# GpSimd starts the second chunk's weight low part only behind VectorE's eight low parts of the norm, in both transitions of a one-core decoder kernel

## What is computed

```python
x = x + rmsnorm(mix, prm['g_post_mix'][layer])
h = rmsnorm(x, prm['g_pre_ffn'][layer])
f = swiglu(h, prm['w_gate_d'][i], prm['w_up_d'][i], prm['w_down_d'][i])
x = x + rmsnorm(f, prm['g_post_ffn'][layer])
if layer == N_A_LAYERS - 1:
    kv = rmsnorm(x, prm['g_kv']) @ prm['w_kv']
```

## Time and profile before

| | |
|---|---|
| time, median of 3 runs | 1826.3 us (1825.19 to 1826.43) |
| profiled execution: own time, span | 1821.79 us, 1820.0 us |
| granted TensorE clock, mean | 0.957 of full speed |
| TensorE busy (matmuls) | 1693.2 us, 93% |
| VectorE, ScalarE, GpSimd busy | 943.6, 745.8, 539.9 us (52%, 41%, 30%) |
| mean DMA rate | 155 GB/s |

### The profile page before, as it was taken

How to read it: one execution, slowest core, us unless ns; L and a number is a source line. 1 busy time by engine, 2 the same in 40 slices (tenths; PEclk the granted TensorE clock), 3 DMA queues, 4 the chain that set the end, 5 groups by cost and what they waited for, 6 DMA issues and landing times.

```text
span 1820.0 us, 29086 instructions
## 1 busy us (share of the span) xinstructions
PE 1693.2 (93%) x11312; PEld 1537.1 (84%) x11312; DVE 943.6 (52%) x1161; ACT 745.8 (41%) x977; POOL 539.9 (30%) x326
## 2 busy tenths in 40 slices
PE   6898797999999998989898998899999999999988
PEld 5898687999999997889666486899898988989886
DVE  6796534211111001322486423877686776868686
ACT  6354453322222122321355222554454554545454
POOL 1001223355554444242000021352331524324161
PEclk8899888999999999999898999899999999999989
DMA  6623202144445342121532415579799796977961
GB/s 206 123 85 131 70 24 70 47 144 144 144 144 181 103 144 86 47 93 60 193 129 84 151 59 130 175 249 297 205 268 232 227 273 208 290 207 237 252 238 49
DMA packets 346267, 281.96 MB, mean 155 GB/s; under 512 B 9505, under 2 KB 311117, under 8 KB 346055
## 3 DMA queue, kind: packets, MB, share of 16 engines
q1 hardware_dynamic: 324947, 251.09, 47.3%
q10 hardware_dynamic: 18084, 18.14, 3.0%
q0 software_dynamic: 3168, 11.80, 2.1%
HBM read 246.62 MB, written 35.10 MB: 155 GB/s over the span
## 4 chain that ended last, share of the span: by engine, by line
PE 77%; DVE 12%; ACT 5%; issue 3%; DMA 1%; SPq 1%; POOL 1%; ACTq 0%; DVEq 0%; POOLq 0%
PE ps L2331 34%; PE ps L2871 14%; PE ps L2874 6%; PE ps L2317 3%; PE ps L2319 2%; PE ps L2318 2%; PE ps L2898 2%; PE ps L2897 2%; DVE cT L1606 2%; PE ps L2459 2%; DVE wlo L1483 1%; PE ps L2293 1%; PE ps L2283 1%; PE ps L2356 1%; DVE zc L1924 1%
## 5 line engine op out<-in xcount | busy, mean ns | idle before, releaser
L2871 PE MATMUL ps<-ejx,ewh 128*128 128x384 f32 x1408 | 403.0, 360 | 5.5 <-DVE ejx L2114 3.6
L2100 DVE TENSOR_TENSOR ewl<-eraw,ewh 128x2048 fp32r<-128x2048 f32 (+1 forms) x144 | 304.0, 2111 | 156.4 <-ACT ewh L1325 156.3
L1325 ACT ACTIVATE ewh<-eraw 128x2048 fp32r<-128x2048 f32 (+1 forms) x144 | 255.2, 1773 | 259.6 <-PE ps L2874 152.8
L2874 PE MATMUL ps<-ejx,ewl 128*128 128x192 f32 x1408 | 353.1, 251 | 0.0
L2331 PE MATMUL ps<-hh,whi 128*128 128x260 f32 x1504 | 315.5, 292 | 31.8 <-DVE hl L1838 25.0
L2331 PE MATMUL ps<-hh,wlo 128*128 128x260 f32 x1504 | 308.8, 288 | 0.0
L2331 PE MATMUL ps<-hl,whi 128*128 128x260 f32 x1504 | 308.5, 287 | 0.0
L867 POOL TENSOR_TENSOR ea<-eat,ea 128x128 fp32r<-128x128 f32 x88 | 176.3, 2003 | 378.5 <-ACT ea L1383 378.4
L2871 PEld LDWEIGHTS ps<-ejx,ewh 128*128 128x128 f32 x1408 | 265.2, 188 | 8.8 <-issue 8.8
L2331 PEld LDWEIGHTS ps<-hh,whi 128*128 128x128 f32 x1504 | 240.3, 194 | 35.4 <-issue 24.8
L2874 PEld LDWEIGHTS ps<-ejx,ewl 128*128 128x128 f32 x1408 | 269.8, 192 | 0.0
(11 more groups left out here) (437 smaller groups left out, 2627.3 us busy)
## 6 DMA issues: line engine op xcount, KB each, us to landing
eraw<-in_w_gate_e SPq DMA_DIRECT2D x88, 512.0 KB, 4.8
eraw<-in_w_up_e SPq DMA_DIRECT2D x88, 512.0 KB, 6.2
eraw<-in_w_down_e SPq DMA_DIRECT2D x64, 512.0 KB, 6.0
eraw<-in_w_down_e SPq DMA_DIRECT2D x48, 256.0 KB, 2.8
xs<-zero ACTq DMA_DIRECT2D x10, 1152.0 KB, 4.8
raw<-in_w_gate_d SPq DMA_DIRECT2D x22, 512.0 KB, 4.0
raw<-in_w_up_d SPq DMA_DIRECT2D x22, 512.0 KB, 5.2
raw<-in_w_down_d SPq DMA_DIRECT2D x16, 512.0 KB, 4.5
```

The source lines that it names most:

```text
L1325: e.activation(ewh[:, s, 0:n], eraw[:, u % RAW, 0:n], ACT.Copy).then_inc(ew_hi, 1)
L2100: e.tensor_tensor(ewl[:, s, 0:n], eraw[:, u % RAW, 0:n], ewh[:, s, 0:n].bitcast(F32), ALU.subtract)\
L2871: e.matmul(ps[:, q, 0:2 * C], ewh[:, s, o:o + P], ejx[:, k, :, :].rearrange("p h n -> p (h n)"), start=(k == 0), stop=(k == KD - 1), skip_ ...
L2874: ins = e.matmul(ps[:, q, C:2 * C], ewl[:, s, o:o + P], ejx[:, k, 0, :], start=False, stop=(k == KD - 1), skip_group_check=True)
```

## The change

Two waits are added to GpSimd's program, one ahead of the loop that begins with the first transition's second chunk, one ahead of the loop that begins with the second transition's. `n_lo` counts VectorE's `hl` tiles; KD is 8. At `n_lo` = 8 the first transition's low parts are all written, at 16 the second's.

```diff
@@ -805,6 +805,7 @@
                 e.tensor_tensor(out=actl[:, bass.ds(i * 2 + j, 1), :], in0=tmp[:, 2 + j:3 + j, :],
                                        in1=acth[:, bass.ds(i * 2 + j, 1), :].bitcast(F32), op=ALU.subtract).then_inc(ga_lo, 1)
 
+            e.wait_ge(n_lo, KD)
             with e.Fori(0, KF // 2) as i:
                 for j in range(2):
                     lo_of_at(U_GU + j + 1, i, 2)
@@ -812,6 +813,7 @@
             with e.Fori(0, 2) as i:
                 for j in range(6):
                     lo_of_at(U_DN + j + 1, i, 6)
+            e.wait_ge(n_lo, 2 * KD)
             with e.Fori(0, 3) as i:
                 for j in range(2):
                     lo_of_at(U_KV + j + 1, i, 2)
```

## The result

| | before | changed |
|---|---|---|
| time, median | 1826.37 us (1825.19 to 1827.57, 4 runs) | 1813.26 us (1809.73 to 1815.0, 4 runs) |
| ratio | | 0.9927, 95% interval 0.9915 to 0.994 |
| span of the profiled execution | 1820.0 us | 1813.2 us |

The change makes the kernel 13.1 us faster, where 8.5 us were forecast and the range ended at a gain of some 12 us. The direction was right, the size was not.

A forecast was written before the change was run, and what follows sets the result against it. TensorE, busy 93% of the span, was taken to bound the kernel, with two 9.8 us waits for `hl`. 2 x 4.25 = 8.5 us off 1826.3 gave 1817.8 us; range 1814.5 to 1821.4 us.

The forecast's parts named there:

- step (1): First transition: without GpSimd's low part beside it, VectorE's third product falls from 5.00 to 0.75 us, 4.25 us less.
- step (2): First chunk: TensorE sets the pace and isn't held again, so the whole 4.25 us arrives.
- steps (3) to (6): Second chunk's low part moves to where VectorE idles, 6.1 us cover; loads and waits cost nothing; second transition gains 4.25 us.
- rival "slower": Second chunk's start: its low part becomes TensorE's last wait, one us per us in each transition; chance 0.02.
- step (7): TensorE's clock in both transitions: same half-speed start expected, term set to zero; bounds 3.6 us either way.
- The base: Forecast counted from the timed runs' median, 1826.3 us, not the profiled execution's 1821.79 us, which was 4.5 us faster.

The follow-up runs named there:

- e9: Kernel before, with 19 matmuls of ones by zeros in TensorE's gap and 4 behind the last squares, in both transitions; 1819.2 us, ratio 0.9961.
- e10: Changed kernel, with 10 matmuls of ones by zeros in TensorE's shorter gap and 4 behind the last squares; 1810.04 us, ratio 0.9919.
- e4: Changed kernel, with seven unused VectorE reductions ahead of the third product in both transitions (8.4 us of stall added); 1826.91 us, ratio 1.0007.
- e7: Changed kernel plus a third wait, for n_lo = 24, at the third series of low parts; 1810.06 us, ratio 0.991.
- e8: Changed kernel, with three unused VectorE reductions ahead of the third product in both transitions (3.6 us of stall added); 1815.86 us.
- e12: Changed kernel, with five unused VectorE reductions ahead of the third product in both transitions (6.0 us of stall added); 1819.39 us.
- e3: Kernel before, with only the wait ahead of the second transition's second chunk; 1817.62 us, ratio 0.995.
- e2: Kernel before, with only the wait ahead of the first transition's second chunk; 1818.36 us, ratio 0.9954.

## Why the prediction was wrong in size

**The stall and its removal, step (1): right.** Product 0.67 us on the chain, TensorE's wait 5.6 us, and with the clock held up 4.25 and 4.26 us in the two transitions, e9 against e10. e4 gives it back, e7 removes the third one.

**The gain arrives whole, step (2): right** for VectorE and the matmuls; the transitions lose a little to the clock, below.

**Where the low part goes, steps (3) to (6): right.** GpSimd starts 0.26 us behind the last `hl` (0.2 were expected), VectorE's next instruction and TensorE's second chunk find it long done, the loads come in time. The rival "slower" never came near; covers of 5.4 and 6.2 us were 5.3 and 6.1 in the forecast.

**The clock, step (7): the step that failed.** The prediction set this term to zero, "so I expect the same half-speed start", and bounded only the half-speed *start* of each transition. The start was as expected and a little worse: the first 24 matmuls take 4.86 to 5.04 us in the first transition of the four changed profiles and 4.60 to 4.68 before. In the second transition they take 4.71 to 4.81 us, and 4.60 to 4.62 before. That is why the transitions gain 3.9 and 4.1 us, not 4.25. But the same rows showed a second half-speed stretch, 334 to 337, which the text names and never prices, and a third near 580 was not looked at. These are the ones that moved. Behind the first root the stretch is gone in all four profiles of the changed kernel, near 580 it is half as long, and the part between is 2.6 us shorter each time. The sum was 2 x 4.25; it should have been 2 x 4.25 less 0.5 plus 2.6, 10.6 us.

Setting the term to zero left out what the clock does beyond the start, and the prediction allowed that the stretches need not hold in other executions. In the profiles they hold. The part between repeats within 0.1 us in four profiles of the stalled version (e4 with them) and in five of the other (e7 with them). Each kernel has its pattern of half-speed stretches behind the first transition, and the pattern changes with the length of TensorE's pause (e8, e12, e4) and when the pause is filled (e9, e10). That it went in the change's favour was not foreseen: in e10 it went the other way. The bounds of 3.6 us either way were wide enough for these 2.1 us, and 10.6 us alone would give 1815.7 us, inside the range. The other 2.5 us of the 13.1 are in no part that the profiles fix. With 11.0 us over all executions they look like scatter of a median of four, which is an estimate and not shown.

**The base.** Taking the median of the timed runs and not the faster profiled execution was right: two more profiles of the kernel before had spans of 1825.1 and 1824.0 us. Of their distance to the first, 5.1 and 4.0 us, 3.4 us each lie in the part behind and the rest ahead of the first transition.

## What to carry to other kernels

Look for single instructions that take several times their median, and read what GpSimd does at that moment. In this kernel GpSimd's operation belonged where VectorE is idle. The wait that put it there cost nothing, since 6.2 us of cover were left, and took 4.25 us off the stall each time.

A gap on TensorE had two prices here: its length, and the half-speed stretches that it left, at its end, 24 us and 270 us later. So price every half-speed window that the profile shows behind the gap, as present and as absent, before the range is drawn. A gap cut in part may pay more than its share, as the last 2.4 us did here (4.0 us in the sum of the three parts), or less. Filling a gap with idle matmuls is a quick way to separate the two, if one of them has been measured first. And look at more executions than the profiled one: in e3 and e9 it lay 6 us off the median.

## What the runs showed that was not expected

- The price of a stall in the transitions is not proportional: 3.6, 6.0 and 8.4 us of added stall cost 3.4, 6.8 and 10.8 us from the first transition to the second, the last step by a half-speed stretch more.
- The clock's pattern behind a pause repeats from profile to profile: 386.35 to 386.41 us for the part between in six profiles (the four of the changed kernel, e2 and e7), 388.89 to 389.02 in five (three of the kernel before, e3, e4).
- A matmul of plain fp32 operands, 128 by 128 by 260 columns, takes 0.44 us and stands as two records in the trace (84 for 42); 12 matmuls of L2331, on the matmul's own type, take 1.44 us, 0.12 us each.
- Matmuls of ones by zeros hold the clock up: 1.00 from 303 to 310 in e9, where it was 0.51.
